# Three matmuls of a filler tile, ahead of or behind the mask in a loop over samples

## The reference

```python
h = rms_norm(x, g_norm1) * (1.0 + sc1) + sh1          # sc, sh, gt from silu(c) @ w_ada
proj = h @ w_in                                        # q | k | v | glu_a | glu_b | gate_a | gate_c
attn = moba_attention(q, k_all, v_all, pos0, slopes) @ w_attn_proj
u = glu_a * sigmoid(glu_b)
cv = silu(layer_norm(depthwise_causal_conv(u, w_dwconv) + b_dwconv)) @ w_conv_proj
mix = (sigmoid(gate_a) * attn + sigmoid(gate_c) * cv) @ w_out
x = x + gt1 * mix
x = x + gt2 * ((silu(f_g) * f_u) @ w_ffn_out)          # f_g, f_u = split(h2 @ w_ffn_in)
```

## Time and profile before

| | |
|---|---|
| median of 3 runs | 586.44 us (585.78 to 588.15) |
| profiled execution | 585.78 us, span 584.0 us |
| TensorE matmul busy | 523.6 us, 90% of the span |
| VectorE busy | 394.2 us, 67% |
| ScalarE busy | 292.1 us, 50% |
| GpSimd busy | 170.0 us, 29% |
| mean granted TensorE clock | 0.958 of 2.4 GHz |

### The profile page before, as it was taken

The page is one execution under the profiler, slowest core; times in us unless marked ns, Lnnn a source line. Parts: engine busy times, 40 slices in busy tenths (PEclk is TensorE's granted clock), DMA queues, the critical chain, the costliest instruction groups (busy, mean ns, idle before and its releaser), DMA issues.

```text
span 584.0 us, 10410 instructions
## 1 busy us (share of the span) xinstructions
PE 523.6 (90%) x4180; PEld 441.1 (76%) x4180; DVE 394.2 (67%) x602; ACT 292.1 (50%) x519; POOL 170.0 (29%) x232
## 2 busy tenths in 40 slices
PE   3769899988979879798798999899999999999997
PEld 3658678865655646556458888799999999999996
DVE  1742674789999998999765865567565656554441
ACT  3144433587777877655653532293444444434331
POOL 8326377287778776750100000000000000000000
PEclk9589898897999999999979999999999999999999
DMA  8999459698999999999676989946466446476501
GB/s 306 370 369 388 165 189 346 224 357 296 405 399 397 420 401 416 366 366 414 260 296 245 387 291 374 364 148 213 150 221 206 147 158 164 122 192 169 153 20 38
DMA packets 82128, 159.31 MB, mean 273 GB/s; under 512 B 2573, under 2 KB 61113, under 8 KB 76952
## 3 DMA queue, kind: packets, MB, share of 16 engines
q1 hardware_dynamic: 76256, 89.27, 45.8%
q0 software_dynamic: 5120, 67.71, 28.9%
q10 hardware_dynamic: 703, 1.67, 0.8%
HBM read 156.39 MB, written 2.72 MB: 272 GB/s over the span
## 4 chain that ended last, share of the span: by engine, by line
PE 57%; DVE 21%; DMA 10%; issue 5%; ACT 4%; POOL 1%; SPq 1%; ACTq 1%; DVEq 0%; POOLq 0%
PE acc L1580 12%; PE acc L1581 12%; PE acc L1582 12%; DVE prod L1057 7%; DMA wring<-in_w_in 6%; DVE sall L1064 4%; PE acc L1452 3%; DMA wring<-in_w_ffn_in 2%; PE acc L1465 2%; PE acc L1467 2%; PE acc L1466 2%; DMA pr<-in_page_table 2%; PE acc L1384 2%; PE chain L1604 2%; ACT L623 1%
## 5 line engine op out<-in xcount | busy, mean ns | idle before, releaser
L1129 DVE TENSOR_TENSOR wlo<-wring,whi 128x1024 fp32r<-128x1024 f32 (+2 forms) x84 | 92.0, 1097 | 72.2 <-ACT whi L623 71.4
L623 ACT ACTIVATE whi<-wring 128x1024 fp32r<-128x1024 f32 (+2 forms) x84 | 80.1, 958 | 83.2 <-PE acc L1582 77.4
L1580 PE MATMUL acc<-xlo,whi 128*128 128x264 f32 x384 | 110.2, 287 | 3.5 <-DVE wlo L1129 1.3
L1581 PE MATMUL acc<-xhi,wlo 128*128 128x264 f32 x384 | 108.8, 283 | 0.0
L1582 PE MATMUL acc<-xhi,whi 128*128 128x264 f32 x384 | 108.8, 283 | 0.0
L578 POOL TENSOR_TENSOR cvT<-cvT,cprod 128x256 f32<-128x256 f32 x120 | 87.9, 732 | 42.4 <-ACT cprod L623 27.6
L1452 PE MATMUL acc<-hT,wring 128*128 128x264 f32 x336 | 92.1, 418 | 3.7 <-DMA wring<-in_w_in 3.3
L1580 PEld LDWEIGHTS acc<-xlo,whi 128*128 128x128 f32 x384 | 72.3, 188 | 5.8 <-issue 3.1
L1452 PEld LDWEIGHTS acc<-hT,wring 128*128 128x128 f32 x336 | 63.3, 200 | 17.6 <-DMA wring<-in_w_in 3.7
L1064 DVE TENSOR_REDUCE sall<-prod 128x32 f32<-128x2048 f32 x32 | 73.0, 2281 | 0.4
L1581 PEld LDWEIGHTS acc<-xhi,wlo 128*128 128x128 f32 x384 | 72.4, 188 | 0.1
(11 more groups left out here) (316 smaller groups left out, 913.4 us busy)
## 6 DMA issues: line engine op xcount, KB each, us to landing
wring<-in_w_ffn_in SPq DMA_DIRECT2D x22, 1024.0 KB, 7.7
wring<-in_w_ada SPq DMA_DIRECT2D x20, 1024.0 KB, 15.3
wring<-in_w_in SPq DMA_DIRECT2D x12, 1024.0 KB, 11.3
wring<-in_w_ffn_out SPq DMA_DIRECT2D x16, 704.0 KB, 5.6
more<-in_w_out SPq DMA_DIRECT2D x4, 1024.0 KB, 13.7
more<-in_w_ada SPq DMA_DIRECT2D x4, 1024.0 KB, 12.5
wring<-in_w_in SPq DMA_DIRECT2D x6, 512.0 KB
wring<-in_w_in SPq DMA_DIRECT2D x4, 768.0 KB
```

The lines of the kernel that those rows point to most:

```text
L623: return nc.scalar.activation(out, in_, f, **kw)
L1129: v.tensor_tensor(wlo[:, place, 0:n, :], w, whi[:, place, 0:n, :].bitcast(F32), ALU.subtract)\
L1580: mm(bank[:, 0:R], whi[:, place, k - k0, :], lo[:, k, :], start=k == 0, stop=False)
L1581: mm(bank[:, 0:R], wlo[:, place, k - k0, :], hi[:, k, :], start=False, stop=False)
```

## The change

The last four matmuls of `THIRD[b-1]` were in two parts, three (`k` 4 to 6) ahead of the mask and one (`k` 7) behind it. Now all four are behind it. Passes 1 to 6 have them; passes 0 and 7 are as they were.

```diff
                 else:
                     split("a1")
 
-                if b - 1 in THIRD:
-                    tile(THIRD[b - 1], mix, 2, hT, k0=4, k1=7)
-
                 pe.wait_ge(pen_ready, b + 1)
                 blocks = pen[:, :, :].rearrange("p (c e) h -> p e c h", e=QU)
                 mm(mask_, posal[:, 0, :], posal[:, 1, :], start=True, stop=False)
...
                 ins.then_inc(mask_ready, 1)
                 if b - 1 in THIRD:
-                    tile(THIRD[b - 1], mix, 2, hT, k0=7)
+                    tile(THIRD[b - 1], mix, 2, hT, k0=4)
                 if b == 0:
                     split("b1")
```

## The result

The changed kernel took 591.7 us (median of 17 runs, 588.3 to 596.3), the kernel before 587.2 us beside it (17 runs, 584.6 to 605.6). The ratio is 1.0065, with an interval from 1.0039 to 1.0093: slower by 0.65%, 3.8 us on the 586.44 us of the table. It is taken over runs in the faster of the chip's two states alone, so it isn't quite the quotient of the two medians. I had forecast 588.4, half of that distance, and had called "same" the likeliest; slower by over 0.5% had 0.35.

A forecast was written before the change was run, and what follows sets the result against it. VectorE sets the pace, busy 23.60 of 24.00 us a pass. Clock and weight terms of passes 1 to 6, 0.9 + 0.35 + 1.0 - 1.0 + 0.4 + 0.2 = 1.85 us, about 2, take 586.44 to 588.4 us; range 585.2 to 591.5.

The forecast's parts named there:

- "same": Whole kernel: time within about 0.5% (2.9 us) of no change, between 583.5 and 589.4 us; chance 0.60.
- Part 1: Mask: it waits for the penalties anyway, so it starts at the same moment without the three matmuls ahead; gain 0.
- Part 2: Behind the mask: four matmuls fit TensorE's 1.42 us idle time before the turn, 0.1 us to spare; direct cost 0.
- Part 3: Third tile: full 1.3 us later, absorbed by ScalarE's 1.56 us of idle time; cost at full clock 0.
- Part 4: TensorE near the mask, passes 1 to 6: clock falls to 1.2 GHz for 3 to 6 us; sum 1.85 us.
- The wait of pass 4 for its weights: Pass 4, L1224: weights land in time, the 1.5 us wait becomes 0.5; taken -1.0, bounds -1.5 to +2.5.
- The step that led there: Ahead of the mask: pass 1's clock fell after 1.38 us idle; the new gap is longer, so all six passes fall.
- Two of my signs: VectorE idle at L1224 in passes 1, 2, 3 and 5, 0.3 to 1.3 us each; turn never waited for.
- The rival of the page: TensorE ahead of the mask: L1611 cuts the gap to 0.5 and 1.7 us, clock stays up; about 587.0; chance 0.17.
- Late weights: Weight loads: asked for later, pass 4 keeps its 1.5 us wait and adds up to 2.5; 591.7 us; chance 0.23.

The follow-up runs named there:

- the run with copies ahead: Changed kernel plus full-width copies of the three moved matmuls ahead of the mask in passes 1 to 6, results thrown away; ratio 0.9972 to the kernel before.
- the run with four ahead: All four matmuls ahead of the mask and none behind, where the kernel before has three and one; ratio 1.0034 to the kernel before.
- the run with pass 6 as before: Changed kernel with pass 6 alone back to three matmuls ahead of the mask and one behind; ratio 1.0087 to the kernel before.
- The kernel before with the second queue: Kernel before, with the second part of weight loads mix2 to mix6 asked for by ScalarE in place of SyncE; ratio 1.0003.
- the narrow copies: Changed kernel plus three copies of the moved matmuls ahead of the mask, 8 columns wide in place of 264; ratio 1.0073 to the kernel before.
- those of pass 7: The run with copies ahead plus five copies in pass 7: three behind the mask, one behind the turn, one behind the prompt's transposes; ratio 0.9981.
- copies behind: Kernel before (three ahead, one behind) plus two copies behind the mask in passes 1 to 6 and five in pass 7; ratio 0.9944.
- the one with one matmul ahead: One matmul ahead of the mask and three behind, where the changed kernel has none and four; ratio 1.0016 to the kernel before.

## Why the prediction was right and wrong

*Part 1, the mask gains nothing:* right. It waits for the penalties in all six passes, now for 1.5 us (1.2 in pass 6).

*Part 2, the moved work fits behind the mask at full clock:* right. In the run with copies ahead the eight instructions took 2.05 us and the turn followed without a wait.

*Part 3, the later tile costs nothing at full clock:* right by the same run. Its wait of 1.0 us in pass 3 was the weights'; such a wait came in one pass each of the kernel before, of that run and of the run with four ahead, in passes 4, 3 and 5.

*Part 4, the clock falls in passes 1 to 6:* right, six of six, and again in the five passes that keep the changed order in the run with pass 6 as before. Full clock with the wide copies showed that the fall is the cause of the loss. The wait of pass 4 for its weights went as forecast.

*The step that led there was weaker than it looked.* I took the 1.38 us of idle time ahead of L1611 for what made pass 1 lose its clock. The kernel before with the second queue has TensorE's list unchanged and the same idle time there, and its clock stays up in pass 1:

```profile
133.02 1.05 PE L1624 MATMUL psT<-headof,pvm 128*128 128x2 f32 x8 [1.39 <-ACT pvm L625]
...
138.53 2.01 PE L1465 MATMUL acc<-hT,wring 128*128 128x264 f32 x8
```

It falls in pass 2 instead, from 163 to 167, behind 0.51 us ahead of L1611. So in the order of before the pass that loses its clock changes from execution to execution, and one trace's pass 1 could not carry a rule for six passes. That all six fell is what the runs showed; that I read it off this row was in part luck.

*The size of part 4 was off:* +1.85 us against +5.27 in the profiled loop and +3.8 by the ratio. Three terms make up the difference. First, I priced each fall as pass 4's, over after eight instructions, while I had pass 1's of 6 us before me; three of the six lasted about 7 us. A long one kept the gate tile slow as well: in pass 6 it was read at 274.9, 10.3 us after the mask's start, in place of 7.7, and cost 2.07 where I had 0.2. In the narrow copies, with the long falls in the odd passes, VectorE waited 1.9 to 2.3 us in each of those. Second, in passes 2 and 4 VectorE waits 0.7 us at L1099 for ScalarE's read of the third tile. I had L1224 as the only reader that minds, and left L1099 out of the sum. Third, pass 4's replacement of the weights' wait was worth 0.5, not 1.0, for the same reason. In pass 1, where I had bounds of 0.45 and 1.3 and took 0.9, it was 0.71. Two of my signs failed as well: pass 5 shows no wait at L1224, and the turn was waited for in pass 6, for 0.2 us.

*The rival of the page* (the clock stays up, since no single idle time is long) had 0.17 and fell: the longest idle time ahead of the masks is 1.5 us, and the clock fell each time. With the narrow copies the idle time right ahead of the masks is 0.84 us or less, and it fell six times of six again. The rule of the Trainium skill, "TensorE: Matmul & The Clock Gate", "Why this matters for your kernels", is about single long gaps; here short gaps with narrow matmuls between them did the same.

*Late weights* (0.23) didn't come with the change: its profile has no wait of TensorE for them. The profiles that have one (the kernel before, copies ahead with and without those of pass 7, four ahead, copies behind) have it in one pass each, 1 to 4 us long; the others have none.

## What to carry to other kernels

Filler on an engine that isn't the bound can still be worth its place: ask of each filler which gap it fills, and what else lies in that gap. Here a tile cut so that three of its matmuls stood ahead of the mask kept TensorE's clock up in most passes, though they hid no latency; whether filler hides latency and whether it holds the clock are two questions, answered by different rows. When a fall of the clock is in a trace once, price it by the longest such fall that the trace has, don't take the pass where it lies for its cause before a second trace agrees, and follow every reader of the late result, not only the tightest one.

## What was not expected of the hardware

Useless matmuls can pay. Copies whose result is thrown away cost nothing that the times show, and ahead of the mask they kept the clock up in passes 1 to 6: the changed kernel went from 1.0065 to 0.9972, and the order of before with copies behind the mask and in pass 7 reached 0.9944.

The kernel is noisy by itself, and not in the loop alone. Pass 0 starts when VectorE gets its first page sums, and that moment differs by some 6 us between profiled executions. First the changed kernel, then the one with one matmul ahead:

```profile
104.30 0.16 DVE L1160 COPY gsT<-small 128x4 f32<-128x4 f32 x1 [8.33 <-PE small L1618]
```

```profile
110.62 0.16 DVE L1160 COPY gsT<-small 128x4 f32<-128x4 f32 x1 [11.39 <-PE small L1618]
```

No edit of this study touches anything ahead of it. A difference of single spans of two such executions (3.2 us here) is therefore no measure of a change in the loop; lengths of passes are.
